# Seven products: weight sums and remainders from ScalarE copies and adding transfers

## What is computed

```python
ffn = (jax.nn.silu(u2 @ w_ffn_gate[layer]) * (u2 @ w_ffn_up[layer])) @ w_ffn_down[layer]
h = h + gate2 * ffn
...
return rms_norm_2(h, final_g)
```

## Time and profile before

| | |
|---|---|
| median of the runs | 1447.18 us |
| the profiled execution: its time | 1450.37 us |
| its span (first to last instruction) | 1449.0 us |
| TensorE busy | 1438.1 us (99% of the span) |
| VectorE busy | 946.3 us (65%) |
| ScalarE busy | 787.4 us (54%) |
| GpSimd busy | 203.3 us (14%) |
| seven products on TensorE, first to last | 1221.15 to 1286.02 us |

### The profile page before, as it was taken

One profiled execution on the slowest core, in us unless ns is written; L12 is line 12 of the kernel. 1 busy time (PEld: TensorE's weight loads), 2 busy tenths in 40 slices (PEclk: granted clock), 3 DMA queues, 4 the chain that ended last, 5 costly groups with the idle time before them and its releaser, 6 DMA issues.

```text
span 1449.0 us, 18874 instructions
## 1 busy us (share of the span) xinstructions
PE 1438.1 (99%) x7172; PEld 1192.3 (82%) x7172; DVE 946.3 (65%) x1720; ACT 787.4 (54%) x1095; POOL 203.3 (14%) x199
## 2 busy tenths in 40 slices
PE   9999999999999999999999999999999999999998
PEld 8888888888888888888888877776888888988887
DVE  7888854365695958466477667847877655862333
ACT  6698897645665647543444565597365333332331
POOL 1111111111111111100002421121010002300001
PEclk9999999999999999999999999999999999999999
DMA  8787887899999998873348566896486432242321
GB/s 257 185 200 180 207 203 186 210 303 310 303 251 251 249 226 227 200 239 119 108 167 293 191 168 166 205 341 211 153 203 189 132 111 72 93 144 89 89 86 59
DMA packets 87227, 274.42 MB, mean 189 GB/s; under 512 B 10128, under 2 KB 14480, under 8 KB 87136
## 3 DMA queue, kind: packets, MB, share of 16 engines
q1 hardware_dynamic: 62832, 190.95, 39.1%
q0 software_dynamic: 21056, 76.62, 27.5%
q10 hardware_dynamic: 3248, 5.64, 1.1%
HBM read 177.62 MB, written 17.83 MB: 135 GB/s over the span
## 4 chain that ended last, share of the span: by engine, by line
PE 91%; DVE 4%; ACT 3%; DMA 1%; issue 1%; DVEq 0%; SPq 0%; ACTq 0%
PE ps L812 28%; PE ps L815 28%; PE ps L813 28%; DVE wlo L2376 1%; DMA raw<-in_ws 1%; ACT pl_f L1683 1%; PE ps L1054 0%; PE ps L1073 0%; PE ps L928 0%; PE ps L1165 0%; PE ps L939 0%; DVE pl_f L2676 0%; ACT wlo L1368 0%; DVE pl_f L2667 0%; DMA wlo<-raw 0%
## 5 line engine op out<-in xcount | busy, mean ns | idle before, releaser
L812 PE MATMUL ps<-pl_r,whi 128*128 128x512 f32 x1870 | 732.6, 392 | 0.2 <-DMA wlo<-raw 0.2
L815 PE MATMUL ps<-pl_r,whi 128*128 128x512 f32 x1870 | 727.9, 389 | 0.0
L813 PE MATMUL ps<-pl_r,wlo 128*128 128x512 f32 x1870 | 727.8, 389 | 0.0
L812 PEld LDWEIGHTS ps<-pl_r,whi 128*128 128x128 f32 x1870 | 351.1, 188 | 77.2 <-issue 3.6
L815 PEld LDWEIGHTS ps<-pl_r,whi 128*128 128x128 f32 x1870 | 351.0, 188 | 73.7 <-DVE pl_r L1835 0.4
L813 PEld LDWEIGHTS ps<-pl_r,wlo 128*128 128x128 f32 x1870 | 351.1, 188 | 72.0 <-issue 0.5
L1359 ACT ACTIVATE whi<-raw 128x1024 fp32r<-128x1024 f32 x234 | 246.9, 1055 | 163.5 <-PE ps L815 128.9
L2827 POOL DMA_DIRECT2D wlo<-raw x146 | 126.4, 866 | 828.5 <-ACT wlo L1368 808.0
L1368 ACT ACTIVATE wlo<-raw 128x1024 fp32r<-128x1024 f32 x146 | 152.8, 1046 | 0.0
L2380 DVE TENSOR_TENSOR wlo<-raw,whi 128x1024 fp32r<-128x1024 f32 x86 | 107.3, 1253 | 41.6 <-ACT whi L1359 41.5
L2750 DVE TENSOR_TENSOR pl_f<-ps,pl_f 128x512 f32<-128x512 f32 x20 | 13.8, 692 | 115.7 <-PE ps L815 115.7
(11 more groups left out here) (320 smaller groups left out, 1408.2 us busy)
## 6 DMA issues: line engine op xcount, KB each, us to landing
raw<-in_w SPq DMA_DIRECT2D x233, 512.0 KB, 4.6
wlo<-raw POOLq DMA_DIRECT2D x146, 512.0 KB, 6.5
pl_f<-in_mod SPq DMA_DIRECT2D x48, 512.0 KB, 7.6
pl_f<-tab SPq DMA_DIRECT2D x12, 512.0 KB, 7.0
raw<-in_ws SPq DMA_DIRECT2D x16, 384.0 KB, 3.9
xs<-pl_f SPq DMA_DIRECT2D x16, 256.0 KB, 7.3
tab<-pl_f SPq DMA_DIRECT2D x8, 512.0 KB, 6.5
pl_f<-xs SPq DMA_DIRECT2D x16, 256.0 KB, 5.7
```

Of the source, the lines that this page charges most:

```text
L812: matmul(out, wh, sr(pair, kk, "hi"), start=start, stop=False)
L813: matmul(out, wl, sr(pair, kk, "hi"), start=False, stop=False)
L815: mm = matmul(out, wh, sr(pair, kk, "lo"), start=False, stop=stop)
```

## The change

Three of the five sums (products 2, 3 and 6 in the new numbering) are begun by ScalarE, which copies one quarter, or minus it, into the sum's buffer; a transfer issued by GpSimd then adds the other quarter onto it. The remainders of products 0 and 1 are made the way of the other streams, by ScalarE's negative copy and an adding transfer. GpSimd computes no sum any more. VectorE makes the sum of product 5 in a buffer, and that of product 4 (A12+A11) in place over the raw quarter A12, once the sum of product 3, which reads A12, is there. VectorE makes five remainders a pass in place of seven. The products are in another order (A11+A22 is now product 2, A12-A22 product 3, A12+A11 product 4), A21 is loaded before A12, and the conditions on which a `raw` buffer is loaded again are new.

```diff
+BY_VECTOR = [..., *(h for h in range(188, NHIS) if not (0 <= h - STR_AT < 7 * NPASS and (h - STR_AT) % 7 < 2))]
-A11, A22, A12, A21 = range(4)
+A11, A22, A21, A12 = range(4)
...
+BEGUN = {2: (A11, 1.0, A22), 3: (A22, -1.0, A12), 6: (A11, -1.0, A21)}
+BEGUN_AFTER = {2: -2, 3: -1, 6: 0}
+SUM_HOME = {2: ("ssum", 0), 3: ("ssum", 1), 6: ("ssum", 2), 5: ("ssum", 3)}
...
 def scalar_engine(k, A):
+    def sums_begun(u):
+        for c, (first, sign, _) in BEGUN.items():
+            if combo_of(u - BEGUN_AFTER[c]) and combo_of(u - BEGUN_AFTER[c])[1] == 0:
+                q = combo_of(u - BEGUN_AFTER[c])[0]
+                A.wait_ge(at("raw", quarter_place(q, first)))
+                A.wait_ge(*([at("w_lo", combo_place(q - 1, c))] if q else freed(*SUM_HOME[c])))
+                act(k.combined(q, c), k.quarter(q, first), ACT.Copy, scale=sign).then_inc(
+                    *done.tick(("begun", q, c)))
...
 def vector_engine(k, V):
     def combined(q, c):
+        V.wait_ge(at("raw", quarter_place(q, first)), at("raw", quarter_place(q, second)))
+        if c == 4:
+            V.wait_ge(at("ssum", q, 3))
...
     def seven_step(h):
+        if combo_of(h):
+            q, c = combo_of(h)
+            if c == 1:
+                combined(q, 5)
+            elif c == 2:
+                combined(q, 4)
+        if h in BY_VECTOR:
+            subtracted(h)
...
 def gpsimd_engine(k, P):
     def combined(q, c):
-        tt(k.combined(c), k.raw[:, first % NRAW, 0:SW], k.raw[:, second % NRAW, 0:SW],
-           ALU.subtract if c in TAKEN_FROM else ALU.add).then_inc(*done.tick(("ssum", q, c)))
+        other = BEGUN[c][2]
+        P.wait_ge(at("begun", q, c), at("raw", quarter_place(q, other)))
+        P.eng.dma_start(k.combined(q, c), k.quarter(q, other), accum_op=ALU.add).then_inc(
+            *k.sum_in[c].tick(("ssum", q, c)))
+
+    def remainder(q, c):
+        h = combo_place(q, c)
+        P.wait_ge(at("w_neg", h))
+        P.eng.dma_start(k.wlo[:, h % NLO, 0:SW].bitcast(F32), k.combined(q, c),
+                        accum_op=ALU.add).then_inc(*k.w_lo[h % NLO].tick(("w_lo", h)))
     for q in range(NPASS):
-        for c in BY_POOL:
-            combined(q, c)
+        combined(q, 2)
+        combined(q, 3)
+        remainder(q, 0)
+        combined(q, 6)
+        remainder(q, 1)
...
 def sync_engine(k, Q):
     def used_up(r):
+            if s == A11:
+                h = combo_place(q, 0)
+                Q.wait_ge(at("w_lo", h), at("w_hi", h), at("begun", q, 2), at("begun", q, 6),
+                          at("ssum", q, 4))
+            elif s == A22:
+                h = combo_place(q, 1)
+                Q.wait_ge(at("w_lo", h), at("w_hi", h), at("ssum", q, 2), at("begun", q, 3),
+                          at("ssum", q, 5))
+            elif s == A21:
+                Q.wait_ge(at("ssum", q, 5), at("ssum", q, 6))
+            else:
+                h = combo_place(q, 4)
+                Q.wait_ge(at("w_lo", h), at("w_hi", h), at("ssum", q, 3))
```

More of the change, by code:

```diff
@@ L28 @@
 NHIS = NUNIT + 7 * NPASS
-BY_VECTOR = [2, *range(114, 138), *range(140, 146), *range(169, 177), 185, *range(188, NHIS)]
+BY_VECTOR = [2, *range(114, 138), *range(140, 146), *range(169, 177), 185,
+             *(h for h in range(188, NHIS) if not (0 <= h - STR_AT < 7 * NPASS and (h - STR_AT) % 7 < 2))]
 BLK_DOWN = 888
-A11, A22, A12, A21 = range(4)
-COMBOS = [((A11,), "bz", 1, "b", 1), ((A22,), "bz", 0, "b", 0), ((A11, A12), "by", 1, "a", 1),
-          ((A11, A22), "bu", 0, "d", 0), ((A21, A22), "bx", 0, "c", 0), ((A12, A22), "by", 0, "a", 0),
+A11, A22, A21, A12 = range(4)
+COMBOS = [((A11,), "bz", 1, "b", 1), ((A22,), "bz", 0, "b", 0), ((A11, A22), "bu", 0, "d", 0),
+          ((A12, A22), "by", 0, "a", 0), ((A12, A11), "by", 1, "a", 1), ((A21, A22), "bx", 0, "c", 0),
           ((A21, A11), "bx", 1, "c", 1)]
-TAKEN_FROM = (5, 6)
-BY_POOL = (3, 5, 6)
-SUM_HOME = {2: ("ssum", 0), 3: ("ssum", 1), 4: ("ssum", 2), 5: ("ssum", 3), 6: ("ssum", 0)}
+BEGUN = {2: (A11, 1.0, A22), 3: (A22, -1.0, A12), 6: (A11, -1.0, A21)}
+BEGUN_AFTER = {2: -2, 3: -1, 6: 0}
+SUM_HOME = {2: ("ssum", 0), 3: ("ssum", 1), 6: ("ssum", 2), 5: ("ssum", 3)}
 def hi_place(u):
@@ L357, in ps, with quarter, combined @@
         return self.banks[self.bank[name]]
-    def combined(self, c):
+    def quarter(self, q, s):
+        return self.raw[:, quarter_place(q, s) % NRAW, 0:SW]
+    def combined(self, q, c):
+        if c < 2 or c == 4:
+            return self.quarter(q, COMBOS[c][0][0])
         return self.sb(*SUM_HOME[c])[:, 0:SW]
@@ L1365, in rounded_weights @@
             rounded_half(u)
[L1366 to L1369, removed]
+            if u not in BY_VECTOR:
+                w = SW if combo_of(u) else UB * 128
+                raw = k.combined(*combo_of(u)) if combo_of(u) else k.raw[:, u % NRAW, :]
+                act(k.wlo[:, u % NLO, 0:w], raw, ACT.Copy, scale=-1.0).then_inc(
+                    *k.w_neg.tick(("w_neg", u)))
+            sums_begun(u)
     def weights(n):
@@ L2373, in subtracted @@
             q, c = combo_of(u)
[L2374 to L2377, removed]
+            tt(k.wlo[:, u % NLO, 0:SW], k.combined(q, c), k.whi[:, u % NHI, 0:SW].bitcast(F32),
+               ALU.subtract).then_inc(*done.tick(("w_lo", u), *[SUM_HOME[c]] if c in SUM_HOME else []))
             return
@@ L2661, in combined @@
     def combined(q, c):
[L2663 to L2666, removed]
-        tt(k.combined(c), k.raw[:, first % NRAW, 0:SW], k.raw[:, second % NRAW, 0:SW],
-           ALU.add).then_inc(*done.tick(("ssum", q, c)))
+        first, second = COMBOS[c][0]
+        V.wait_ge(at("raw", quarter_place(q, first)), at("raw", quarter_place(q, second)))
+        if c == 4:
+            V.wait_ge(at("ssum", q, 3))
+        else:
+            last = combo_place(q - 1, c)
+            V.wait_ge(*([at("w_hi", last), at("w_lo", last)] if q else freed(*SUM_HOME[c])))
+        tt(k.combined(q, c), k.quarter(q, first), k.quarter(q, second), ALU.add).then_inc(
+            *done.tick(("ssum", q, c)))
     into = {m: at("x", 5, m) for m in range(8)}
@@ L2823, in halves @@
         for u in due:
[L2824 removed]
+            if u in BY_VECTOR or combo_of(u):
                 continue
```

36 lines of the change are left out of this document (7 added, 29 removed).

## The result

| | median, us | lowest to highest | runs |
|---|---|---|---|
| before, beside it | 1447.27 | 1446.45 to 1447.44 | 4 |
| changed kernel | 1455.21 | 1454.75 to 1455.49 | 4 |

The ratio is 1.0056 (95% interval 1.0038 to 1.0073): **slower by 7.9 us**, where +4.0 was forecast. The profiled execution of the changed kernel took 1455.45 us, span 1454.1.

A forecast was written before the change was run, and what follows sets the result against it. TensorE, busy 99% of the span, was taken as the bound, so only its idle time counted: -4.2 + 7.3 + 0.9 = +4.0 us on the median 1447.18, giving 1451.2 us, range 1445.8 to 1456.8.

The forecast's parts named there:

- The hole at product 1 of passes 1 to 3: TensorE standing still about 2.3 us before product 1, waiting for its remainder's adding transfer behind other transfers.
- 3.7 us alone, 2.0 us of the engines for 384 KB: Each added 384 KB adding transfer: lands 3.7 us after issue if alone, occupies the DMA engines for 2.0 us.
- the rival built on it: Faster, chance 0.08: adding transfers as quick as plain loads, 3.0 us; remainder 1 in time, no hole left, 1443.0 us.
- 3 x 2.3 + 0.4: New TensorE stalls before product 1 of three passes, plus 0.4 for the last pass's 512 KB unit: 7.3 us.
- I add 0.9 us in all for partly late ones: Allowance of 0.9 us for next-pass quarter loads landing late, chiefly A12, which sum 3 wants at 11.0.
- 4.2 us as all that this stretch can give back: TensorE's three old holes at passes' first products, over the seven products, taken as the most to win: 4.2 us.
- The forecast case: The main case, chance 0.42: the changed kernel slower by +2.9 to +6.5 us.
- late quarters at every boundary: Rival, chance 0.20: A12 takes 7.6 us, delaying products 0 and 1; 1454.8 us, with a third such boundary 1456.6.
- three boundaries of 0.85 us: Range's lower end: somewhat shorter transfers, each pass boundary costing 0.85 us, given as 2.8 against 4.2; 1445.8 us.
- three of 1.8 on top of 1451.2: Range's upper end: late quarters cost 1.8 us more at all three pass boundaries; given as 1456.8 us.
- Because GpSimd is slow to let go of them, and the two engines then stretch each other: Explanation of the old holes: quarters reload late behind GpSimd's sums, and VectorE is stretched, 2.65 us against 0.95.
- Edits at nothing: VectorE's in-place sum for product 4 and the new product order priced at zero, with 5 us of cover.

The follow-up runs named there:

- e1: Changed kernel with the remainders of products 0 and 1 made by VectorE again, the three begun sums kept; 1445.30 us, 0.9985 of the kernel before.
- e5: Changed kernel with only product 1's remainder made by VectorE again, product 0's still by adding transfer; 1446.03 us, 0.9992 of the kernel before.
- e2: Changed kernel with GpSimd issuing sum 6 after remainder 1 instead of ahead of it; 1448.98 us, 1.0012 of the kernel before.
- e3: Changed kernel with the load of the next A11 also waiting for remainder 1; 1453.90 us, 1.0045 of the kernel before.
- e4: Changed kernel with GpSimd's queue ordered sum 2, remainder 0, sum 3, remainder 1, sum 6; 1449.84 us, 1.0015 of the kernel before.
- e0: The kernel before, unchanged, run for a second profile; median 1446.84 us, ratio 1.0000.
- e6: Changed kernel without adding transfers: GpSimd computes sums 2, 3, 6, VectorE all remainders, new product order kept; 1445.83 us, 0.9990 of the kernel before.
- e9: Kernel of e6 with sum 6 written to sum 2's buffer, as in the kernel before; 1447.06 us, 0.9999 of the kernel before.
- e8: Changed kernel with both remainders issued ahead of sums 3 and 6, VectorE's in-place sum behind product 2's remainder; 1448.14 us, 1.0008 of the kernel before.
- the repeat: The changed kernel, unchanged, run for a second profile; median 1454.44 us over 3 runs, 1.0046 of the kernel before.

## Why the prediction was right or wrong

**Direction and mechanism: right.** The hole at product 1 of passes 1 to 3, ended by `wlo<-raw`, came as told. e1 (both remainders away) and e5 (remainder 1 away) remove it, e2 (sum 6 behind it) too, and e3 shows that 0.8 to 1.0 us of it is the A11 load and the rest the queue.

**3.7 us alone, 2.0 us of the engines for 384 KB: right.** Lone transfers landed after 3.8 us at best, and transfers in line landed 2.0 us apart (e4). Scaling with the bytes was the right choice. The Trainium skill's fit on the page "DMA: Bandwidth & Descriptors", section "Anatomy of one DMA", gave an estimate of 2.9 us for this size; no adding transfer of any run was that quick, and the rival built on it did not come.

**"3 x 2.3 + 0.4": 7.3 us, measured 6.78.** The 0.4 for the last pass did not show (2.28 there, 2.16 in pass 2).

**"I add 0.9 us in all for partly late ones": 1.15 measured** in the first execution and 0.64 in the second, in pass 1 alone. The size was right by luck. The prediction looked for them behind a stall, with A12 landing at 11 to 13; there A12 landed at about 9.5 (4.3 and 4.4 us after its issue), and product 0 was in time. The late one is at the first boundary, which has no stall before it. Holes together: 8.2 forecast, 7.93 and 7.42 measured.

**"4.2 us as all that this stretch can give back": the term that was mis-sized.** It was read from one execution, 3.2 us above the median, and then taken off the median. The text said how the execution stood to the median, and did not draw the conclusion that its holes might be part of the 3.2. The second execution had 2.0 us. This is 2.2 us of the 4.0 by which the forecast fell short.

**The clock: not in the sum.** Another 1.5 us. The execution of before kept a clock of 0.999 over its span, and the prediction counted only idle time. The forecast case ended at +6.5. That the range goes on to 1456.8 and holds the measured 1455.2 is luck: its upper part stood for late quarters at every boundary, and what filled it were this term and the one before.

**The sum with both put right:** the stages lie 2.2 us (e0) and 9.7 us above the 60.48 of their matmuls: -2.2 + 9.7 = +7.5 us, against +7.9 measured.

**Two sums in the range:** three boundaries of 0.85 us are 2.55, not 2.8, which puts the lower bound at 1445.5; three of 1.8 on top of 1451.2 give 1456.6, not 1456.8. Neither changes anything here.

**"Because GpSimd is slow to let go of them, and the two engines then stretch each other": half right.** GpSimd is indeed late, but by its wait for the shared buffer and not by its speed. With its sums kept and sum 6 in its own buffer (e6) the holes go, with the shared buffer (e9) they return in part. The stretching is real (2.65 us), and costs nothing while the quarters are early (e6); once they are late, the stretched instruction is what TensorE waits for (e9).

**Edits at nothing:** the cover of the in-place sum held here (it waited 1.93 us in pass 1 and started 1235.11, before TensorE wanted it). Where sum 3 was moved back, in e8, it became the link that made the next passes late, by 0.8 and 1.7 us. The prediction had priced it only at product 2's remainder, not at the reload of A11 behind it.

## What to carry to other kernels

In these runs, work that moved from an engine to a DMA queue took its latency plus everything ahead of it on that queue (3.8 us alone, some 2.0 more for each transfer still ahead of it). Move what has slack longer than that (the sums here, and product 0's remainder), and leave on the engine what is wanted within a few microseconds (product 1's remainder); e1 keeps three of the five transfers and beats both kernels, 0.9985 of the time before. Before a stall of one profiled execution is counted as gain, ask where that execution stands among the runs: if it is above the median, its stall may be why. And a change that bundles a reordering with new means is best judged part by part: 1.6 of the 1.8 us that were to be won here came without any transfer, nearly all of it with one more buffer, which the sum in place had freed.

## What was not expected of the hardware

- TensorE's granted clock fell to the 1.2 GHz level for about 3.4 us after holes of 1.15 and 2.34 us with one product between them, and of 0.64 and 2.33 in the repeat. It did not fall after single holes of 2.2 to 2.3 us in passes 2 and 3, nor after 1.40 and 1.52 in e3. What exactly makes it fall wasn't isolated. The cost, 1.5 us, is as much as a whole hole of e3.
- GpSimd issues a transfer 0.53 us after the one before it, though each shows as 0.86 (1231.14, then 1231.67 in the changed kernel's timeline), so the issuing was not what spaced the landings 2 us apart.
- The same code had stage lengths of 62.64 and 64.87 us in two executions of the kernel before, and of 69.63 and 70.16 us in two of the changed one. The other kernels were profiled once each, so whether their stages vary less isn't shown.
